# A MoE block kernel on one Trainium2 core: four width classes of the expert tiles (128, 136, 148, 160) instead of three

## The reference

```
hf = rmsnorm(h).reshape(1024, 1024)
logits = hf @ w_router + b_router              # 32 experts
top_vals, top_idx = lax.top_k(logits, 4)       # each token goes to 4 experts
gates = softmax(top_vals)
order = argsort(top_idx.reshape(-1))           # 4096 (token, expert) pairs, by expert
xs = hf[order // 4]
sizes = bincount(top_idx.reshape(-1), length=32)
gu = ragged_dot(xs, w_gate_up, sizes) + b_gate_up[e_sorted]    # 1024 -> 2048
gate = minimum(gu[:, :1024], 7.0)
up = clip(gu[:, 1024:], -7.0, 7.0)
act = (up + 1.0) * (gate * sigmoid(1.702 * gate))
out = ragged_dot(act, w_down, sizes) + b_down[e_sorted]        # 1024 -> 1024
y = segment_sum(out * gates, order // 4)
```

## Time and profile before

| | |
|---|---|
| time, median of 3 runs | 2291.48 us (2290.32 to 2299.23) |
| the profiled execution: its own time | 2284.88 us |
| its span, first to last instruction | 2283.0 us |
| mean granted TensorE clock | 0.966 |
| expert tiles on TensorE | 725.0 to 2238.0 us |
| TensorE busy | 2123.9 us, 93% |
| GpSimd, VectorE, ScalarE busy | 558.1, 730.0, 404.3 us |
| transfers | 486.70 MB, mean 213 GB/s |

### The profile page before, as it was taken

The page is one execution under the profiler, slowest core; times in us unless marked ns, Lnnn a source line. Parts: engine busy times, 40 slices in busy tenths (PEclk is TensorE's granted clock), DMA queues, the critical chain, the costliest instruction groups (busy, mean ns, idle before and its releaser), DMA issues.

```text
span 2283.0 us, 42195 instructions
## 1 busy us (share of the span) xinstructions
PE 2123.9 (93%) x15622; PEld 1923.6 (84%) x15623; DVE 730.0 (32%) x1930; ACT 404.3 (18%) x1018; POOL 558.1 (24%) x637
## 2 busy tenths in 40 slices
PE   6999997899984899999999999999999999999992
PEld 5888885455544899999999999999999999999992
DVE  0222222333323233433233332333333333343331
ACT  1221212323211111111111111111111111111110
POOL 1122221010022223223322332222232322323321
PEclk9999998999986999999999999999999999999996
DMA  7000004212104889999998999999999989999997
GB/s 271 10 18 9 9 1 147 56 28 56 29 19 143 263 261 323 315 291 290 296 294 273 310 296 289 299 289 288 271 302 311 315 262 273 315 316 314 301 289 85
DMA packets 305781, 486.70 MB, mean 213 GB/s; under 512 B 106786, under 2 KB 128162, under 8 KB 305698
## 3 DMA queue, kind: packets, MB, share of 16 engines
q1 hardware_dynamic: 249394, 441.14, 59.2%
q0 software_dynamic: 33120, 44.91, 9.4%
q10 hardware_dynamic: 23232, 0.18, 0.6%
HBM read 454.81 MB, written 35.84 MB: 215 GB/s over the span
## 4 chain that ended last, share of the span: by engine, by line
PE 88%; DVE 3%; issue 3%; SPq 1%; ACT 1%; DMA 1%; POOL 1%; ACTq 0%; DVEq 0%; POOLq 0%
PE psum L975 41%; PE psum L991 22%; PE psum L798 7%; PE psum L940 5%; PE psum L811 2%; PE psum L889 1%; PE psum L846 1%; PE psum L814 1%; PE psum L888 1%; PE psum L923 1%; PE psum L852 1%; PE psum L906 1%; PE psum L952 1%; DMA area<-in_x 1%; DVE area L1289 1%
## 5 line engine op out<-in xcount | busy, mean ns | idle before, releaser
L975 PE MATMUL psum<-area 128*128 128x128 f32 (+2 forms) x8192 | 994.4, 284 | 40.9 <-issue 23.1
L975 PEld LDWEIGHTS psum<-area 128*128 128x128 f32 x8192 | 985.7, 192 | 46.4 <-issue 46.3
L991 PE MATMUL psum<-area 128*128 128x128 f32 (+2 forms) x4096 | 502.8, 284 | 1.6
L991 PEld LDWEIGHTS psum<-area 128*128 128x128 f32 x4096 | 491.2, 191 | 10.7 <-DVE area L1289 9.9
L1270 DVE TENSOR_SCALAR area<-psum,area 128x160 f32<-128x160 f32 x256 | 86.5, 379 | 628.5 <-PE psum L975 628.5
L575 POOL DMA_INDIRECT sum_rows<-area x165 | 261.8, 1587 | 67.3 <-issue 40.2
L737 ACT ACTIVATE area<-area 128x320 f32<-128x320 f32 x128 | 60.2, 470 | 754.2 <-DVE area L1270 754.2
L798 PEld LDWEIGHTS psum<-area 128*128 128x128 f32 x1536 | 176.2, 194 | 3.8 <-issue 3.3
L798 PE MATMUL psum<-area 128*128 128x128 f32 x1536 | 177.6, 277 | 0.0
L565 POOL DMA_INDIRECT area<-normed_rows,area x165 | 160.5, 972 | 62.1 <-issue 61.8
L560 POOL TENSOR_TENSOR area<-area 128x5 uint32<-128x5 uint32 x33 | 6.2, 189 | 644.4 <-DVE area L1255 607.1
(11 more groups left out here) (187 smaller groups left out, 1273.4 us busy)
## 6 DMA issues: line engine op xcount, KB each, us to landing
area<-in_w_gate_up SPq DMA_DIRECT2D x256, 1024.0 KB, 6.3
area<-in_w_down SPq DMA_DIRECT2D x128, 1024.0 KB, 6.9
area<-in_x SPq DMA_DIRECT2D x16, 512.0 KB, 4.0
area<-in_w_in SPq DMA_DIRECT2D x1, 4096.0 KB, 12.9
area<-in_w_o SPq DMA_DIRECT2D x1, 4096.0 KB, 13.7
sum_rows<-area SPq DMA_DIRECT2D x32, 128.0 KB, 2.7
normed_rows<-area SPq DMA_DIRECT2D x8, 512.0 KB, 2.8
out<-sum_rows SPq DMA_DIRECT2D x4, 1024.0 KB, 13.8
```

What stands on the lines that cost most here:

```text
L975: ins = mm(dst, w_gu[piece][:, k, c * P:(c + 1) * P], xT[:, PART * s + k, 0:width], start=(s == 0 and k == 0 and c % 2 == 0), stop=(s == 1 ...
L991: ins = mm(bank[4 + d // 3][:, (d % 3) * SLOTS:(d % 3) * SLOTS + width], w_dn[q][:, kk, d * P:(d + 1) * P], actT[:, 2 * q + kk, 0:width], ...
```

## The change

The list of widths gets a fourth entry, and the two middle ones move:

```diff
-WIDTHS = [P, P + 16, SLOTS]
+WIDTHS = [P, P + 8, P + 20, SLOTS]
```

## The result

The changed kernel takes 2274.53 us (median of 4 runs, 2273.29 to 2275.32), the kernel before beside it 2292.83 (4 runs). The ratio is 0.9919, with a 95% interval of 0.9901 to 0.9936: 14.7 to 22.7 us faster, about 18.3. The sum on record was -18.6 us, and 2273. The total holds; how it comes about does not, and most of what follows is on that.

The account below looks back on a forecast made before the run. TensorE's streaming in the expert tiles was taken as the bound. Columns -17.5, comparisons +2.4 and code loads -3.5 sum to -18.6 us, from 2291.5 to 2273 us, range 2260 to 2284.

Parts of the forecast that it names:

- What bounds it: Expert tiles are bound by TensorE's own streaming, busy 93% of the span; the weight queue waits for TensorE.
- Columns: Expert tiles at new widths 136 and 148 stream 64 columns fewer in all: -17.5 us.
- As three points lie on a line I take the line: Half-tile times at 128, 144, 160 columns give 0.27 us a column, so whole tiles cost 45.76 at 136, 49.05 at 148.
- The bound of -21.8: Lower bound of the columns term, if tile time were proportional to width, 0.34 us a column.
- Code loads: TensorE's waits for 16 KB code packets at the ends of tiles 0, 1 and 6: together -3.5 us.
- The straddled border: Packet border between the two L145 loop-end instructions causes two waits after tile 0; one remains after the change, -3.5 us.
- The wait after tile 6: First run of the 148 copy fetches packet 22 anew and the jump goes there: one wait more, +6.1 us.
- After tile 1 nothing touches 22: The 136 copy fetches packet 20 only, so the idle 4.35 us after tile 1 shrinks and clock stays up: -6.1 us.
- a packet entered first fetches the one behind it, held or not: Code-load rule: first entry after a packet's load fetches its successor, and whoever needs that meanwhile waits; gave -3.5 us together.
- Rival 3: Jump to loop's end drops loaded code until copies run unbroken; tiles 1 to 6 end waiting, +12 to +39 us, chance 0.09.
- Comparisons: The four 148 and four 160 tiles make one more comparison at L1018, 0.3 us each: +2.4 us.
- the two-page window: Skill's rule that taken branches outside two pages fetch 16 KiB, at all 31 tile ends; given no chance of its own.

Follow-up runs that it names:

- the moved code: Kernel before with four more instructions ahead of TensorE's loop, so both L145 loop-end instructions lie behind a packet border; 2284.22 us, a single execution.
- empty pass: Changed kernel plus one pass of TensorE's loop before tile 0 making all comparisons but running no copy; 2260.53 us, 0.9859 of the kernel before.

## Why the prediction came out as it did

Term by term, from the two traces; whole tiles are taken start to start, less the idle time shown before the next (47.80 us at 144 and 52.26 at 160 before; 45.18 at 136 and 48.81 at 148 after).

| term | predicted | in the trace | where |
|---|---|---|---|
| six tiles 144 to 136 | -13.1 | -15.7 | 6 x (45.18 - 47.80) |
| two tiles 144 to 148 | +2.2 | +2.0 | 2 x (48.81 - 47.80) |
| two tiles 160 to 148 | -6.6 | -6.9 | 2 x (48.81 - 52.26) |
| wait before tile 1 | -3.5 | -3.6 | 6.26 - 9.85 |
| wait before tile 2, and its low clock | -6.1 | +0.3 | 5.02 - 4.35, 16.41 - 16.78 |
| wait before tile 7, and its low clock | +6.1 | +6.1 | 4.57, 16.02 - 14.46 |
| low clock of tile 1 | 0 | +0.7 | 17.85 - 15.09 against 18.04 - 15.94 |
| other tile ends | +2.4 | -0.5 | 13.0 - 4.57 against 8.9 |
| tile 0, clock at its start | 0 | -1.1 | 16.01, 7.83 against 17.50, 7.41 |
| sum | -18.6 | -18.7 | measured -19.0 |

**What bounds it** was right. In no run does TensorE wait for a weight transfer in the tiles, and in the changed kernel the queue that issues the weights still waits for TensorE for 673.7 + 372.6 us of the 1346 from 884 us on.

**Columns** were mis-sized: -20.6 us where the prediction took -17.5. The step that failed is "As three points lie on a line I take the line". They lie nearly on one by chance; 128 lies at the end of a floor, and 136 costs 22.53 us a half where the line has 22.88. The bound of -21.8, from proportional columns, holds the -20.6, but it is no true bound: from 144 to 136 a half falls by 1.44 us, 0.18 a column, where the proportional price is 0.17. Reckoned as the prediction did, twice the first half, the term is -22.7 us and outside it; the second halves are 0.1 us dearer at 136 and cheaper at 144, and the table has them in.

**Code loads.** The straddled border (two waits after tile 0) was right and is shown by the moved code. The wait after tile 6, at the first run of the 148 copy, came where it was put, at its size. What failed is "After tile 1 nothing touches 22". The changed kernel's sequencer shows it from 828 to 840 us, against the earlier trace rows:

```profile
L145 PEldq FUSED_REGOPS  x2: 37/50/64, 837.4 to 837.7; - x2
L145 PEldq COMPARE_BRANCH  x1: 232/232/232, 837.5 to 837.5; - x1
L1018 PEldq COMPARE_BRANCH  x2: 83/2616/5150, 832.2 to 838.6; - x2
```

The branch that leaves the copy takes 5150 ns: packet 22, held since tile 0, was gone. The rule "a packet entered first fetches the one behind it, held or not" does not explain this. With the addition that a load drops what lies ahead it fits the waits of both kernels and of the other traces that I followed, but for the missing load of packet 22 in the kernel before. Rival 3 had this mechanism, but too strong: the end is dropped only when a new packet comes in, so tiles 2 to 5 do not wait. The term is +3.5 us instead of -3.5, low clock of tile 1 included.

**Comparisons.** The prediction charged 2.4 us for them and overlooked that the border cost something at every tile's end. With the code moved and three copies as before, the waits from 882 us on are 5.7 us; in the changed kernel they are 8.4. So the comparisons cost about 2.7, close to the 2.4, and the border gives back 3.2. Tile by tile the 2.7 us lie where they should: before the eight tiles that make one comparison more (6, 8, 10, 13, 16, 18, 23 and 24) the wait is 0.17 to 0.67 us longer than with the moved code, before the others it differs by 0.01 at most.

So three errors, -3.1, +7.0 and -2.9 us, leave +1.0, and tile 0's clock, chance, takes 1.1 off. The total was right by luck, by their cancelling, and the change is worth what it is for the widths: 17.7 us where code loads are out of the way.

**What is kept.** Of the rule in the Trainium skill, "Runtime: NRT & Kernel Launch", section Instruction fetch mechanics, the two-page window is refuted here: no packet in 1155 us of jumps over up to three copies in the changed kernel. Its 128 KiB for TensorE agree with the break between seven packets (26 loads) and nine (85).

## What to carry to other kernels

Copies of a loop's body for different sizes save only what lies above the size at which the engine's cost leaves its floor, so measure the price at sizes between those you know before drawing a line through them. And count the code: a loop that jumps over copies is cheap only as long as all of it stays loaded. Here first visits to copies made the loop's end wait for code again, three times with a low clock behind it, and an empty pass in rising order during idle time took that away. A total that comes out right is no proof of its terms; read each of them in the trace after.

## What the runs showed of the hardware

- A code packet is 16 KB (0.38 MB in 23). In the changed kernel a jump to one that is not held stops TensorE's sequencer for 5.0 to 6.1 us at a branch; the engine idles 4.6 to 6.3 us, and the stage behind runs 1.6 to 2.8 us longer, at a mean granted clock of 0.84 to 0.90 instead of 1.00 (columns as in the earlier trace rows; the stages of tiles 1 and 7):

```profile
786.20:804.10 17.90, 17.90 (x129) 17.78 (x130) 5.49 (x15) 3.04 (x7) 1.54 (x2) 0.84 0.53 156
...
1072.00:1088.10 16.10, 16.01 (x129) 15.83 (x129) 5.49 (x15) 3.05 (x7) 1.22 (x2) 0.90 0.62 189
```

- A loop of seven packets is kept, one of nine is not: 26 loads, 22 with the empty pass, and 85, with 99 us more. That loading a packet drops held ones that lie ahead of it is inferred from when TensorE waits and loads.
- A packet border inside the few instructions between two tiles cost 3.2 us over 29 tile ends although no packet was loaded (8.9 against 5.7 us of waits).
- An fp32 half tile costs 21.8 us at each of the widths 112, 120, 124 and 128, and 0.11 to 0.22 us more a column from 132 up.
- Two executions of the same code ahead of the tiles differ by 9 us. The later one is 2.5 us ahead at 370 us and 8.8 behind at 625, in the attention stage, where its granted clock is 0.81, 0.93 and 0.97 in the stretches from 300, 400 and 500 us, against 0.90, 0.97 and 1.00.
